# The scan's steps and running sums made at attention's front; weights through other buffers

## What is computed

```
dt = jax.nn.softplus(dt_raw + dt_bias)
a = -jnp.exp(a_log)
xdt = xs * dt[..., None]
a_cs = jnp.cumsum(dt * a, axis=2)                      # the running sums, within each chunk
lmat = jnp.exp(jnp.where(causal, a_cs[l] - a_cs[s], -inf))
y_diag = einsum(C, B, lmat, xdt)
states = einsum(B, exp(a_cs[-1] - a_cs), xdt);  h = h * exp(a_cs[-1]) + states
y = y_diag + einsum(C, h_prev, exp(a_cs)) + d_skip * xs
s = RMSNorm(y * silu(z), ssd_norm_w)
x_out = x + concat([a_attn * silu(g), s]) @ w_out
```

## Time and profile before

| | |
|---|---|
| median of 3 runs | 2910.41 us (2906.63 to 2915.34) |
| the profiled execution | 2905.6 us, span 2904.0 us |
| busy in the span | PE 2676.4 (92%), DVE 1235.0 (43%), ACT 889.1 (31%), POOL 868.5 (30%) |
| project | 0 to about 1366 us |
| attend | 1366 to about 2148 us |
| scan_a | 2148.65 to about 2607 us |
| finish | to 2904.0 us |

### The profile page before, as it was taken

One profiled execution on the slowest core, in us unless ns is written; L12 is line 12 of the kernel. 1 busy time (PEld: TensorE's weight loads), 2 busy tenths in 40 slices (PEclk: granted clock), 3 DMA queues, 4 the chain that ended last, 5 costly groups with the idle time before them and its releaser, 6 DMA issues. The chain is left out here.

```text
span 2904.0 us, 43635 instructions
## 1 busy us (share of the span) xinstructions
PE 2676.4 (92%) x16598; PEld 2362.2 (81%) x16598; DVE 1235.0 (43%) x3366; ACT 889.1 (31%) x1933; POOL 868.5 (30%) x663
## 2 busy tenths in 40 slices
PE   7899999999999999997899999999926999976999
PEld 7899999999998888884799999999824777764675
DVE  3245555444000015442565666656515555533321
ACT  3312222222111111211355555555614444422000
POOL 1045455512121213121023333333332333321510
PEclk9999999999999999998899999999967999997999
DMA  4224344575223111112444554544344656536851
GB/s 162 80 75 109 107 131 141 146 212 166 80 69 131 58 61 55 73 44 86 150 135 138 150 164 132 169 147 134 90 113 134 194 174 195 175 109 204 310 195 66
DMA packets 197788, 382.26 MB, mean 132 GB/s; under 512 B 61611, under 2 KB 119187, under 8 KB 183732
## 3 DMA queue, kind: packets, MB, share of 16 engines
q1 hardware_dynamic: 156916, 229.77, 26.0%
q0 software_dynamic: 38016, 145.28, 15.4%
q10 hardware_dynamic: 2672, 4.74, 0.5%
HBM read 259.94 MB, written 125.15 MB: 133 GB/s over the span
## 5 line engine op out<-in xcount | busy, mean ns | idle before, releaser
L118 PE MATMUL bank<-w_hi,hT_hi 128*128 128x256 f32 x1792 | 508.1, 284 | 13.7 <-DMA ident<-ident 11.3
L120 PE MATMUL bank<-w_hi,hT_lo 128*128 128x256 f32 x1792 | 504.8, 282 | 0.0
L119 PE MATMUL bank<-w_lo,hT_hi 128*128 128x256 f32 x1792 | 503.3, 281 | 0.0
L118 PEld LDWEIGHTS bank<-w_hi,hT_hi 128*128 128x128 f32 x1792 | 338.8, 189 | 14.6 <-DMA ident<-ident 11.6
L1179 PE MATMUL front<-k_hi,q_st 128*128 128x256 f32 x768 | 317.3, 421 | 30.3 <-DMA k_lo<-qk 23.4
L120 PEld LDWEIGHTS bank<-w_hi,hT_lo 128*128 128x128 f32 x1792 | 339.2, 189 | 0.0
L119 PEld LDWEIGHTS bank<-w_lo,hT_hi 128*128 128x128 f32 x1792 | 338.9, 189 | 0.0
L1222 PE MATMUL obank<-turned_p,v_in 128*128 128x128 f32 (+1 forms) x1632 | 315.3, 326 | 4.9 <-ACT turned_p L1355 4.0
L1342 ACT ACTIVATE score<-score,ntop_sb 128x256 f32<-128x256 f32 (+1 forms) x768 | 290.8, 458 | 5.3 <-DMA ntop_t<-ntop 4.8
L1222 PEld LDWEIGHTS obank<-turned_p,v_in 128*128 128x128 f32 x1632 | 266.8, 194 | 22.0 <-ACT turned_p L1355 5.3
L1180 PE MATMUL front<-k_lo,q_st 128*128 128x256 f32 x768 | 274.7, 366 | 0.0
(11 more groups left out here) (299 smaller groups left out, 4958.4 us busy)
## 6 DMA issues: line engine op xcount, KB each, us to landing
qk<-xc_in SPq DMA_DIRECT2D x64, 512.0 KB, 5.0
w_raw<-w_in POOLq DMA_DIRECT2D x26, 1024.0 KB, 7.6
q_st<-qk POOLq DMA_DIRECT2D x16, 1024.0 KB, 5.3
k_hi<-qk POOLq DMA_DIRECT2D x16, 1024.0 KB, 7.5
k_lo<-qk POOLq DMA_DIRECT2D x16, 1024.0 KB, 9.6
v_in<-v_out POOLq DMA_DIRECT2D x16, 1024.0 KB, 9.5
cum_all<-cum SPq DMA_DIRECT2D x16, 1024.0 KB, 9.7
xcT<-xc SPq DMA_DIRECT2D x12, 1024.0 KB, 3.9
```

The source lines that it names most:

```text
L118: pe.matmul(out, lhs_hi(k), rhs_hi(k), start=k == 0, stop=False)
L119: pe.matmul(out, lhs_hi(k), rhs_lo(k), start=False, stop=False)
L120: last = pe.matmul(out, lhs_lo(k), rhs_hi(k), start=False, stop=k == KT - 1)
```

## The change

In `attend`, the prologue of the scan is made. The three loads (dt, dt_bias, a_log) stand first on SP's queue, the chain of DVE and ACT stands ahead of everything else on these engines, in spare columns of `acc[:, 1, :]`. PE turns the four pieces into `back[0]` between maxima_out(0) and scores(1), DVE copies them after `meet(0, 0)`, and SP stores the sums (after the chain) and the steps with the sums by token (`steps`, 256 KB, after the copies). ACT waits for these stores before it writes `acc[:, 1, :]`.

In `scan_a`, the prologue is gone. SP loads the identity, the first xc, `tok`, tri and the first sums, then d_skip, norm_b, the second sums, z and xc. The weight slabs pass through u (two), part and sq. ACT issues the first four after x_tok of chunk 0, and casts the weights after its own preparation of chunk 0; DVE subtracts after its preparation and d_diag, then applies chunk 0. PE does off, new and diag of chunk 0 ahead of its first product, and prepares chunk 1 between the first and the second. POOL's gate(0) waits for all of w_split.

```diff
@@ attend @@
+        spare = lambda at, n: acc[:, 1, at * P:(at + n) * P]
+        dt_raw, step_h, cum_h, work_a, work_b, tok_flat = (spare(2 * i, 2 if i < 5 else 4) for i in range(6))
+        tok = tok_flat.rearrange("p (a c h) -> p a c h", a=2, h=H)
...
 @block.sync
             sp.sem_inc(stored, 32)
+            sp.dma_start(dt_raw, scr["dtT"].rearrange("h (g t) -> (h g) t", t=2 * P)).then_inc(step_in, 16)
+            sp.dma_start(h_small[:, 0:1], per_head(io["dt_bias"])).then_inc(step_in, 16)
+            sp.dma_start(h_small[:, 1:2], per_head(io["a_log"])).then_inc(step_in, 16)
             sp.dma_start(ident[:, :], io["ident"]).then_inc(const_in, 16)
             load_bias(0)
             load_bias(1)
             load_gate(0)
+            sp.wait_ge(pro_ok, 1)
+            for i in range(2):
+                sp.dma_start(scr["cum"].rearrange("(g i) (h l) -> i h g l", i=2, l=P)[i], cum_h[:, i * P:(i + 1) * P]).then_inc(step_out, 16)
             tops_out(0, 0)
...
             load_bias(2)
+            sp.wait_ge(tok_made, 4)
+            sp.dma_start(scr["steps"], tok_flat).then_inc(step_out, 16)
...
 @block.tensor
             scores(0)
             maxima_out(0)
+            pe.wait_ge(pro_ok, 1)
+            for a, src in enumerate((step_h, cum_h)):
+                for i in range(2):
+                    at = (2 * a + i) * P
+                    last = pe.transpose(back[0][:, at:at + P], src[:, i * P:(i + 1) * P], ident[:, :])
+            last.then_inc(step_turned, 1)
             scores(1)
             maxima_in(0)
+            pe.wait_ge(tok_made, 4)
...
 @block.vector
+            chain = Chain(dve, pro_dve)
+            dve.wait_ge(step_in, 16 * 3)
+            chain(dve.tensor_scalar(dt_raw, dt_raw, h_small[:, 0:1], None, ALU.add))
...
+            dve.tensor_tensor_scan(cum_h, work_a, work_b, 0.0, ALU.mult, ALU.add).then_inc(pro_ok, 1)
             scores(0, 0, 0)
             maxima_out(0)
             scores(1, 1, 0, range(8))
             meet(0, 0)
+            dve.wait_ge(step_turned, 1)
+            turned = back[0][:, :].rearrange("p (a i h g) -> p a i g h", a=2, i=2, h=H)
+            for a in range(2):
+                for i in range(2):
+                    dve.tensor_copy(tok[:, a, :, :].rearrange("p (g i) h -> p i g h", i=2)[:, i], turned[:, a, i]).then_inc(tok_made, 1)
...
@@ scan_a @@
-        slab = lambda k: cum_all[:, :, :, :].rearrange("p b h l -> p (b h l)")[:, (k % SLABS) * D:(k % SLABS + 1) * D]
+        slabs = (u[:, 0, :], u[:, 1, :], part[:, :], sq[:, :])
+        slab = lambda k: slabs[k % SLABS]
...
 @block.sync
+            sp.dma_start(ident[:, :], io["ident"]).then_inc(first_in, 16)
+            load_xc(0)
+            sp.dma_start(tok[:, :, :, :].rearrange("p a c h -> p (a c h)"), scr["steps"]).then_inc(first_in, 16)
+            sp.dma_start(tri[:, :], io["tri"]).then_inc(first_in, 16)
+            load_cum(0)
...
-            sp.wait_ge(w_split, KT)
-            load_cum(0)
             load_cum(1)
...
 @block.scalar, prepare(c)
                 act.copy(x_tok[:, :], XA[:, :]).then_inc(x_taken, 1)
+                if c == 0:
+                    for k in range(SLABS):
+                        load_w(k)
...
             prepare(0)
+            high(0)
+            for k in range(KT):
+                high_w(k)
+                if k + SLABS < KT:
+                    load_w(k + SLABS)
...
 @block.gpsimd, gate(c)
+                if c == 0:
+                    pool.wait_ge(w_split, KT)
...
 @block.vector
             exponents(0)
             prepare(0)
+            dve.wait_ge(small_in, 16 * 3)
+            dve.tensor_tensor(d_diag[:, :, :], spread(d_col[:, :], P), repeat(ident[:, :], KT), ALU.mult).then_inc(diag_made, 1)
+            low(0)
+            for k in range(KT):
+                low_w(k)
+            dve.wait_ge(w_split, KT)
+            apply(0)
             for c in range(NC):
...
                 take_a(2 * c)
-                apply(c)
+                if c >= 1:
+                    apply(c)
...
 @block.tensor
             prepare(0)
-            for c in range(NC):
+            off(0)
+            new(0)
+            pe.wait_ge(diag_made, 1)
+            diag(0)
+            attended(0)
+            prepare(1)
+            attended(1)
+            for c in range(1, NC):
```

More of the change, by code:

```diff
@@ L1320, in mix @@
                         scores(h + 2, b, pair + 1, units_at.get(g, ()), beside=h)
+            chain = Chain(dve, pro_dve)
+            dve.wait_ge(step_in, 16 * 3)
+            chain(dve.tensor_scalar(dt_raw, dt_raw, h_small[:, 0:1], None, ALU.add))
+            chain(dve.scalar_tensor_tensor(out=work_b, in0=dt_raw, scalar=-1.0, in1=dt_raw, op0=ALU.mult, op1=ALU.max))
+            dve.wait_ge(pro_act, 2)
+            chain(dve.tensor_scalar(work_a, work_b, 1.0, None, ALU.add))
+            dve.wait_ge(pro_act, 3)
+            chain(dve.tensor_tensor(step_h, step_h, work_b, ALU.mult))
+            chain(dve.tensor_scalar(work_a, work_a, -1.0, None, ALU.add))
+            chain(dve.scalar_tensor_tensor(out=cum_h, in0=work_a, scalar=0.0, in1=work_b, op0=ALU.is_equal, op1=ALU.mult))
+            chain(dve.tensor_scalar(work_a, work_a, 1e-30, None, ALU.max))
+            chain(dve.reciprocal(work_a, work_a))
+            chain(dve.tensor_tensor(step_h, step_h, work_a, ALU.mult))
+            chain(dve.tensor_tensor(step_h, step_h, cum_h, ALU.add))
+            chain(dve.scalar_tensor_tensor(out=step_h, in0=dt_raw, scalar=0.0, in1=step_h, op0=ALU.max, op1=ALU.add))
+            chain(dve.tensor_scalar(h_small[:, 2:3], h_small[:, 2:3], -1.0, None, ALU.mult))
+            chain(dve.tensor_scalar(work_b, step_h, h_small[:, 2:3], None, ALU.mult))
+            chain(dve.memset(work_a, 1.0))
+            chain(dve.memset(work_a.rearrange("h (c l) -> h c l", l=P)[:, :, 0:1], 0.0))
+            dve.tensor_tensor_scan(cum_h, work_a, work_b, 0.0, ALU.mult, ALU.add).then_inc(pro_ok, 1)
             scores(0, 0, 0)
@@ L1374, in scan_a @@
     HG = H // G
-    SPLIT = P // H
     HALF = 512
@@ L1536, in high @@
                 act.copy(m_hi[:, t % 2, :, :], m_raw[:, t % 2, :, :]).then_inc(m_high, 1)
[L1538 to L1550, removed]
             def square(c):
@@ L1666, in take_a @@
                 dve.tensor_tensor(y_t[:, i % 4, :], acc[:, :], y_t[:, i % 4, :], ALU.add).then_inc(a_out, 1)
[L1668 to L1687, removed]
@@ L1688, in _ @@
-            chain(dve.tensor_scalar(work_b[:, :], step_h[:, :], h_small[:, 2:3], None, ALU.mult))
-            chain(dve.memset(work_a[:, :], 1.0))
-            chain(dve.memset(work_a[:, :].rearrange("h (c l) -> h c l", l=P)[:, :, 0:1], 0.0))
-            dve.tensor_tensor_scan(cum_h[:, :], work_a[:, :], work_b[:, :], 0.0, ALU.mult, ALU.add).then_inc(pro_ok, 1)
-            dve.tensor_tensor(d_diag[:, :, :], spread(d_col[:, :], P), repeat(ident[:, :], KT), ALU.mult).then_inc(diag_made, 1)
-            dve.wait_ge(pro_pe, 1)
@@ L1695, in _ @@
-            turned = MX[:, :].rearrange("p (a i h g) -> p a i g h", a=2, i=2, h=H)
-            for a in range(2):
-                for i in range(2):
-                    dve.tensor_copy(tok[:, a, :, :].rearrange("p (g i) h -> p i g h", i=2)[:, i], turned[:, a, i]).then_inc(pro_ok, 1)
-            low(0)
-            for k in range(KT):
-                low_w(k)
-            dve.wait_ge(pro_ok, 5)
+            dve.wait_ge(first_in, 16 * 3)
             dve.wait_ge(mhalf_set, 2)
@@ L1777, in _ @@
         def _(pe):
-            pe.wait_ge(small_in, 16 * 8)
-            pe.wait_ge(pro_ok, 1)
-            for a, src in enumerate((step_h, cum_h)):
-                for i in range(2):
-                    at = (2 * a + i) * P
-                    last = pe.transpose(MX[:, at:at + P], src[:, i * P:(i + 1) * P], ident[:, :])
-            last.then_inc(pro_pe, 1)
-            pe.wait_ge(pro_ok, 5)
-            pe.wait_ge(diag_made, 1)
+            pe.wait_ge(first_in, 16 * 3)
             def prepare(c):
@@ L2462 @@
     "cum": (TILES, H * P),
+    "steps": (P, 2 * TILES * H),
     "q_s": (NB * H, HD),
```

41 lines of the change are left out of this document (18 added, 23 removed).

## The result

The changed kernel is slower: 2926.5 us (median, 2915.1 to 2931.3) against 2908.5 for the kernel before in the same comparison. The ratio is 1.0054, interval 1.0035 to 1.0073. I had forecast 2899.0. The profiled execution took 2915.06 us, with a span of 2913.4, and it is the shortest of the changed kernel's.

A forecast was written before the change was run, and what follows sets the result against it. PE, busy 92% of the span, was taken as the bound, so only its waits could be won. scan_a's start gains 13.0 us, attention costs 1.5: 11.5 us off the median 2910.41 gives 2898.9, forecast 2899, range 2891 to 2910.

The forecast's parts named there:

- After that point both kernels run the same loop.: scan_a after the third product with w_out: both kernels run the same loop, so no term was summed for it.
- From there the loop is bound by PE, with small waits: scan_a from the first product with w_out (T0+62.5 before; T0 is SP's first load): PE bounds it, small accumulator waits.
- The signs that I had named: Prediction wrong if PE's first transposes (XA) start after T0+16, the split ends after T0+49, or DVE's first score awaits its chain.
- First loads: Start of scan_a: PE's needed inputs landed by T0+12.5, or T0+20.4 if xc lands as late as before.
- ACT's path: Start of scan_a: x_tok from T0+14.6, 8.2 us to the exponential's end plus 1.6 for four weight issues, ending T0+24.4.
- W: End of DVE's weight split in scan_a, forecast at T0+44.7, against T0+51.6 before.
- The rest of the start: scan_a: split 15.5 us, first product 7.6, new wait before the second 12.3, third 11.0 after the second; ends at T0+75.6.
- Attention: Start of attention: later first product +0.6, four copies of tok +0.9, the chain of steps hidden; sum -1.5 us.
- R1: scan_a's first loads are the bound, xc landing at T0+20.4: gain 3.6 us, 2906.8; 18%.
- R2: scan_a: weight slabs land late or both products run at the low clock: gain 5.5 us, 2904.9; 12%.
- R3: Attention: a_log's load stands behind GpSimd's transfers, DVE 17 us late: 5.5 us slower, 2915.9; 8%.
- R5: scan_a: split end moves only 6.9 us and the wait before the second product eats the rest: gain 5.4, 2905.0; 4%.

The follow-up runs named there:

- run 13: The changed kernel repeated unchanged, on one chip with its padded variants: 2924.6 us, 1.0063 to the kernel before.
- Runs 3 and 4: take_a(2c-1) put ahead of exponents(c+1) on DVE in scan_a's loop, on the kernel before (2874.1 us, 0.9900) and on the changed one (2876.9, 0.9910).
- old order: Kernels with exponents(c+1), which waits for cum, ahead of take_a(2c-1) on DVE: 2908.5 us before the change, 2926.5 after.
- new order: Kernels with take_a(2c-1) ahead of exponents(c+1) on DVE: 2874.1 us on the kernel before, 2876.9 on the changed one.
- run 8: Changed kernel with SP's norm_b, cum for chunk 1, z and second xc issued only after b_tok of chunk 0: 2919.5 us, 1.0037.

## Why the prediction was wrong

- **"After that point both kernels run the same loop."** This is the step that failed. The instructions are the same, but their targets moved by an odd 32 bytes, and the loop got 11 us longer in the profiled execution and 21 in that of run 13. My sum had this term at nothing. I never listed what the dropped tensors do to the addresses of the others. With that undone, the change measures 0.9982 to 0.9990 in three comparisons, 3 to 5 us faster, the sign I had forecast and less than half the 11.5 us. In the fourth, with 352 bytes in place of 32, it is 1.0013.
- **"From there the loop is bound by PE, with small waits."** Wrong. The waits of the earlier trace rows are small one by one, but they come in each chunk and end a chain that runs through a load. Runs 3 and 4 moved one call and won 1.0% of the kernel before and 1.4% of the changed one.
- **The signs that I had named** all came: XA after T0+16, the split's end after T0+49, and DVE's first score, at 1389.06, right behind its own chain.
- **First loads.** PE began at T0+16.2, released by tri. I had taken 12.5 and had 20.4 as the other end: +3.7.
- **ACT's path.** From x_tok (T0+18.2) to the exponential's end (T0+32.2) it took 14.0 us, not 9.8: +4.2. I took 1.6 us for four issues, from two on a calm queue, although also had four taking 5.32. They took 6.8. The premise "SP has issued by then" was false, for SP issued until 2171.94. These two terms made W T0+52.4 instead of T0+44.7, no earlier than the old T0+51.6.
- **The rest of the start** held. The split took 15.5 us as forecast. The first product took 7.2 us (7.6), with the clock rising some 3.5 us in. The new wait put the second 13.0 us after the first's end (12.3), of which PE idled 11.31. The third was released 10.0 us after the second (11.0). From W on the forecast error is 0.7 us, against 7.7 up to W.
- **Attention.** I had -1.5 and it is 0. The inputs landed 10.5 us into the stage, released by a_log 9.4 us after its issue (I had 8.3), and the chain ended at 1389.1. DVE's first scores then came late, and PE, which started at 1382.23, waited 5.29 us. But PE had started earlier in its stage than before (13.2 us in, not 18.7), so the two cancelled. I had worked out neither. The first table load ran at 1369.00, ahead of ACT's wait, and cost nothing. The second (1380.79, 1.28 us) stood right behind one function and right ahead of the next (1382.09), and the chain took 9.6 us as before. By the Trainium skill (ScalarE: Activation LUTs, "What ACT_TABLE_LOAD costs"), which puts a drain of some 1.38 us to each load, I had estimated 2.8 us more for this chain; no run here shows that.
- **Rivals.** R1 and R2 were half right each: the first loads and the weights' late issue together took 7.9 us up to W. R3 did not happen. R5 was the nearest: W itself didn't move. None of them ends above 2924, and none had the loop in it.

## What to carry to other kernels

Look for a wait on a load inside a loop's chain, and put what the bound engine needs ahead of it: here one reordered call was worth 1%, and the change itself 0.2% at best. When a change drops or adds a buffer, compare the start of every later transfer target modulo 64 before and after, and pad it back; otherwise the measurement is of the layout and not of the change. Cost an issue by what else is in flight at that moment, since an issue queued in front of an engine's own work is that engine's time.

## What the hardware did that I had not expected

- With SBUF targets that start 32 bytes past a multiple of 64 the loop's loads were slower. In the old order 1 MB of cum landed in 10.5 to 11.2 us (medians), and in 9.6 to 10.3 with every target on such a multiple. GpSimd's packets (m_raw and the x tiles) took more of the engines' time too. Between 2280 and 2520 this is the row of the changed kernel of run 13 (packets, MB, share of the 16 engines' time):

```profile
q0 software_dynamic: 6215, 9.53, 18.6%
```

and with the 32 bytes:

```profile
q0 software_dynamic: 6611, 9.96, 16.4%
```

 That is 75 against 63 us of one engine for each MB (3840 us times the share, by the MB). In the same stretch all five traces with every target off have 71 to 75, and all seven with every target on 63 to 68; in the new order it is 72 against 67 to 69, although the time is the same there. SP's queue, which carries cum, shows hardly any of it (45.8 to 47.0 against 44.9 to 46.4). With cum_all alone put back it is 65.0, with cum_all alone off 67.1: neither alone raises it, and I have no cause for that.

 The Trainium skill (DMA: Bandwidth & Descriptors, "How a descriptor splits into AXI transactions") says that a descriptor is split into transactions of at most 256 bytes, and that where it doesn't start on a multiple of 256 the first one starts at the multiple below, so that bytes which nobody uses cost time too. It tells this of reading; taken for the target as well, an address of 61632 (192 over such a multiple) and one of 56480 (160 over) should cost about alike, and 56832 (0 over) less. The runs show landings of 9.8, 10.9 and 9.9 us, so what goes with the cost here is the odd 32. Which part of the path pays for it stays open.
- An issue on a queue took 8.22 us here (norm_b on SP; 0.34 in run 8, where it was issued some 18 us later), and two took 4.28 (w_out on ACT), while earlier transfers ran. ACT, which issues its own loads, stood still for 5.87 us over it.
- The kernel before had medians from 2898.1 to 2908.5 us in the six comparisons of this study, more than this change is worth.
